# A block stack in float32r on one core: second products of three feed-forward layers rebuilt as seven-product quads, with one weight sum made by an adding transfer

## What is computed

```
# first block, layer i (0, 1): hidden width 4096
h = modulate(rmsnorm(x, norm_g[i, 1]), sh2, sc2)
x = x + gt2 * (square(relu(h @ mlp_w1[i])) @ mlp_w2[i])
# second block, both feed-forwards: hidden width 2816
def swiglu(h, w_gate, w_up, w_down):
    return (silu(h @ w_gate) * (h @ w_up)) @ w_down
x = x + 0.5 * swiglu(rmsnorm(x, ffn_norm), w_gate, w_up, w_down)
```

## Time and profile before

| | |
|---|---|
| median of 3 runs | 2538.02 us (2536.36 to 2540.02) |
| the profiled execution, its own time | 2542.36 us |
| its span, first to last instruction | 2540.6 us |
| mean granted TensorE clock | 0.988 |
| TensorE matmul busy | 2490.3 us (98%) |
| TensorE weight load busy | 2050.9 us (81%) |
| VectorE / ScalarE / GpSimd busy | 1329.9 / 908.6 / 201.8 us |

### The profile page before, as it was taken

How to read it: one execution, slowest core, us unless ns; L and a number is a source line. 1 busy time by engine, 2 the same in 40 slices (tenths; PEclk the granted TensorE clock), 3 DMA queues, 4 the chain that set the end, 5 groups by cost and what they waited for, 6 DMA issues and landing times.

```text
span 2540.6 us, 39183 instructions
## 1 busy us (share of the span) xinstructions
PE 2490.3 (98%) x16966; PEld 2050.9 (81%) x16966; DVE 1329.9 (52%) x1967; ACT 908.6 (36%) x1364; POOL 201.8 (8%) x176
## 2 busy tenths in 40 slices
PE   9999999999999999999999999999999999999998
PEld 7888888876787887888888888888668987888887
DVE  7865746647845446543444544432345745444433
ACT  4224323337633233431433322322256444322221
POOL 1000000000220000000000111000221000111100
PEclk9999999999999999999999999999999999999999
DMA  8563665622210003232222332333112422322232
GB/s 341 192 197 117 200 197 185 189 86 81 85 39 4 5 29 126 82 108 99 93 100 75 108 100 95 91 97 124 64 48 76 141 79 65 114 92 99 87 100 71
DMA packets 79725, 271.86 MB, mean 107 GB/s; under 512 B 8912, under 2 KB 11216, under 8 KB 79040
## 3 DMA queue, kind: packets, MB, share of 16 engines
q1 hardware_dynamic: 67696, 224.79, 26.9%
q0 software_dynamic: 11856, 44.55, 5.5%
HBM read 265.11 MB, written 4.19 MB: 106 GB/s over the span
## 4 chain that ended last, share of the span: by engine, by line
PE 92%; DVE 5%; ACT 2%; issue 1%; DMA 0%; SPq 0%; DVEq 0%; ACTq 0%
PE ps L624 26%; PE ps L630 22%; PE ps L628 22%; PE ps L640 3%; PE ps L643 3%; PE ps L655 1%; DVE WLs L1780 1%; PE ps L796 1%; PE ps L809 1%; DVE ada L1796 1%; PE ps L597 1%; PE ps L822 1%; PE ps L693 1%; PE ps L1119 1%; PE ps L1133 1%
## 5 line engine op out<-in xcount | busy, mean ns | idle before, releaser
L1780 DVE TENSOR_TENSOR WLs<-raw,WHs 128x1024 fp32r<-128x1024 f32 (+2 forms) x406 | 461.4, 1137 | 419.4 <-ACT WHs L1218 418.7
L624 PE MATMUL ps<-HH,WHs 128*128 128x512 f32 x1728 | 646.6, 400 | 3.7 <-DVE Pq L2332 2.1
L1218 ACT ACTIVATE WHs<-raw 128x1024 fp32r<-128x1024 f32 (+2 forms) x424 | 416.7, 984 | 550.7 <-PE ps L630 444.7
L630 PE MATMUL ps<-HH,WLs 128*128 128x512 f32 x1406 | 548.3, 390 | 1.2 <-DVE WLs L1780 1.2
L628 PE MATMUL ps<-HL,WHs 128*128 128x512 f32 x1406 | 547.7, 390 | 0.0
L624 PEld LDWEIGHTS ps<-HH,WHs 128*128 128x128 f32 x1728 | 324.9, 189 | 76.0 <-issue 11.2
L630 PEld LDWEIGHTS ps<-HH,WLs 128*128 128x128 f32 x1406 | 263.9, 188 | 57.2 <-DVE WLs L1780 1.6
L628 PEld LDWEIGHTS ps<-HL,WHs 128*128 128x128 f32 x1406 | 264.4, 188 | 53.7 <-issue 2.2
L624 PE MATMUL ps<-HM,WHs 128*128 128x512 f32 x576 | 224.1, 389 | 0.0
L628 PE MATMUL ps<-HM,WHs 128*128 128x512 f32 x576 | 224.1, 389 | 0.0
L630 PE MATMUL ps<-HM,WLs 128*128 128x512 f32 x576 | 224.1, 389 | 0.0
(11 more groups left out here) (419 smaller groups left out, 3449.0 us busy)
## 6 DMA issues: line engine op xcount, KB each, us to landing
ada<-in_adaw POOLq DMA_DIRECT2D x80, 512.0 KB, 4.5
raw<-in_f1gu_m SPq DMA_DIRECT2D x38, 512.0 KB, 3.3
raw<-in_f2gu_m SPq DMA_DIRECT2D x38, 512.0 KB, 3.2
raw<-in_mw_0b SPq DMA_DIRECT2D x32, 512.0 KB, 3.5
raw<-in_mw_1b SPq DMA_DIRECT2D x32, 512.0 KB, 3.5
raw<-in_w_in_m SPq DMA_DIRECT2D x18, 512.0 KB, 3.3
ada<-in_adaw SPq DMA_DIRECT2D x16, 512.0 KB, 15.7
raw<-in_cw_in_m SPq DMA_DIRECT2D x16, 512.0 KB, 3.4
```

Of the source, the lines that this page charges most:

```text
L624: pe.matmul(o[m], WHs[:, s, w], hi, start=k == 0, stop=False)
L630: t = pe.matmul(o[m], WLs[:, s, w], hi, start=False, stop=k == DEPTH_K[name] - 1)
L1218: act.activation(WHs[:, SLOT[v], 0:n], raw_[:, v % NRAW, 0:n], ACT.Copy).then_inc(*S.up("w_hi", ("hi", v)))
L1780: dve.tensor_tensor(WLs[:, s, 0:n], raw_[:, v % NRAW, 0:n], WHs[:, s, 0:n].bitcast(F32), SUB).then_inc(*S.up("w_lo", ("lo", v)))
```

## The change

The second products of MLP layer 1 and of the feed-forwards are done in quads: two output blocks by two halves of the tokens by two halves of the depth make a 2x2 by 2x2 block product, which is done with 7 products in place of 8 (Strassen's scheme). Each of the 7 has half of the depth and 256 tokens. The layer's hidden width is now cut into parts: `mw1_1` in 12, 10 and 10 blocks ("a", "b", "c"), each followed by its second product; `f1gu` and `f2gu` in 24 and 20 blocks. The new kind is "s"; `f2d_b` alone keeps kind "m", now with depth 10. The rest of the kernel, MLP layer 0 too, stays as it was.

- Input side: for each pair k of hidden blocks VectorE makes four combinations T1 to T4 (256 columns each), in place in the temporaries, and high and low parts of seven 256-column inputs are stored (1792 columns for a pair, before 1024).
- Weight side: the four quarters of a quad are loaded (4 transfers); of the 7 weight pieces three are quarters, three are sums by VectorE (`sum_quarters`, pieces 1, 2, 6), and piece 4 is a quarter to which a second transfer adds another one in SBUF, issued by GpSimd (`added`). Each piece gets its high and low part as before.
- Output side: each of the 7 products is added to X with its sign as soon as it is done (`draw`, 256 columns); three PSUM banks serve a quad, and four of the products are built on top of an earlier one in the same bank (`BEFORE`), after that one was drawn.
- The ring `pr` of the feed-forwards has three places in place of four, and `ending()` works on depth 10.

The code follows in this order: the tables; `fast` of TensorE; `hidden_fast` of ScalarE; the call of `sum_quarters` in VectorE's `ahead`; `combinations` and `hidden_fast` of VectorE; its `residual`, in which the products 5 and 6 of a quad close one output block each; `added` of GpSimd; `ending`.

```diff
-        ("mw1_1a", "e", 16, 8), ("mw2_1a", "m", 8, 16), ("mw1_1b", "m", 16, 8), ("mw2_1b", "m", 8, 16),
-        ("f1gu", "f", 44, 8), ("f1d", "m", 8, 22),
+        ("mw1_1a", "e", 12, 8), ("mw2_1a", "s", 8, 12), ("mw1_1b", "m", 10, 8), ("mw2_1b", "s", 8, 10),
+        ("mw1_1c", "m", 10, 8), ("mw2_1c", "s", 8, 10),
+        ("f1gu_a", "f", 24, 8), ("f1d_a", "s", 8, 12), ("f1gu_b", "m", 20, 8), ("f1d_b", "s", 8, 10),
...
-        ("f2gu", "f", 44, 8), ("f2d", "m", 8, 22)]
+        ("f2gu_a", "f", 24, 8), ("f2d_a", "s", 8, 12), ("f2gu_b", "m", 20, 8), ("f2d_b", "m", 8, 10)]
+BANK = [1, 2, 1, 3, 1, 2, 1]
+BEFORE = {2: 0, 4: 2, 5: 1, 6: 4}
+DRAWS = [(0, 0, 1), (1, 1, -1), (1, 0, -1), (0, 0, 1), (1, 1, -1), (1, 0, -1), (0, 1, 1)]
+INPUT = [0, 3, 1, 5, 2, 4, 6]
+INPUT_GROUP = [0, 2, 1, 3, 1, 2, 3]
+GROUP = [slice(0, 256), slice(256, 768), slice(768, 1280), slice(1280, 1792)]
+SUMMED = (1, 2, 4, 6)
+ADDED = (4,)
...
+            def fast(name):
+                src = name.replace("mw2", "mw1")
+                for a in range(BLOCKS[name] // 2):
+                    o = {}
+                    for i in range(7):
+                        u, b, g = FIRST[name] + 7 * a + i, BANK[i], INPUT_GROUP[i]
+                        if b not in o:
+                            o[b] = bank(name, a, b, hold=True)[:, 0:256]
+                        else:
+                            on.wait_ge(*S.at("drawn", name, a, BEFORE[i]))
+                        s, n = SLOT[u], WANT[u][4]
+                        x = slice(256 * INPUT[i], 256 * INPUT[i] + 256)
+                        on.wait_ge(*S.at("hi", u))
+                        for k in range(n):
+                            w = slice(128 * k, 128 * k + 128)
+                            on.wait_ge(*S.at("ch", src, k, g))
+                            pe.matmul(o[b], WHs[:, s, w], HT[:, 0, k, x], ...)
+                            on.wait_ge(*S.at("cl", src, k, g))
+                            pe.matmul(o[b], WHs[:, s, w], HT[:, 1, k, x], ...)
+                            on.wait_ge(*S.at("lo", u))
+                            t = pe.matmul(o[b], WLs[:, s, w], HT[:, 0, k, x], ...)
...
+            def hidden_fast(name):
+                def finish(m):
+                    k, x = m // 2, tmp_[:, m % 4]
+                    if m % 2 == 0:
+                        on.wait_ge(*S.at("t2", name, m))
+                        high(name, k, 0, x[:, early])
+                    else:
+                        on.wait_ge(*S.at("T4", name, k))
+                        high(name, k, 2, T2[:, 1])
+                        high(name, k, 1, T2[:, 0])
+                        high(name, k, 3, x)
+                def evac(m):
+                    on.wait_ge(*S.at("full", name, m))
+                    if m >= 4:
+                        on.wait_ge(*S.at("cl", name, (m - 4) // 2, 3))
+                    act.activation(tmp_[:, m % 4], taken(name, m), ACT.Relu)...
+                    if m:
+                        finish(m - 1)
+                    if m == BLOCKS[name] - 1:
+                        finish(m)
...
+                    if v + 1 < len(WANT) and WANT[v + 1][1] == "s" and WANT[v + 1][3] in SUMMED and WANT[v + 1][3] not in ADDED:
+                        sum_quarters(v + 1)
...
+            def combinations(src, k, even, odd, t1, t2, t3, t4):
+                dve.tensor_tensor(t3, odd[:, late], even[:, late], SUB)...
+                on.wait_ge(*S.at("T1", src, k))
+                dve.scalar_tensor_tensor(out=t2, in0=t1, scalar=-1.0, in1=odd[:, late], op0=MUL, op1=SUB)...
+                on.wait_ge(*S.at("T2", src, k))
+                dve.scalar_tensor_tensor(out=t4, in0=t2, scalar=-1.0, in1=odd[:, early], op0=MUL, op1=SUB)...
...
+            def hidden_fast(name):
+                def finish(m):
+                    k, x = m // 2, tmp_[:, m % 4]
+                    if m % 2 == 0:
+                        low(name, k, 0, x[:, early])
+                    else:
+                        low(name, k, 2, T2[:, 1])
+                        low(name, k, 1, T2[:, 0])
+                        low(name, k, 3, x)
+                def evac(m):
+                    k, x = m // 2, tmp_[:, m % 4]
+                    on.wait_ge(*S.at("relu", name, m))
+                    dve.tensor_tensor(x, x, x, MUL).then_inc(*S.up("v_evac", ("t2", name, m)))
+                    if m:
+                        finish(m - 1)
+                    on.wait_ge(*S.at("t2", name, m))
+                    if m % 2 == 0:
+                        if k:
+                            on.wait_ge(*S.at("cl", name, k - 1, 1))
+                        first_combination(name, k, x, T2[:, 0, late])
+                    else:
...
+                        combinations(name, k, tmp_[:, (m - 1) % 4], x, T2[:, 0, late], T2[:, 0, early], T2[:, 1, early], T2[:, 1, late])
+                    if m == BLOCKS[name] - 1:
+                        finish(m)
...
+                    if isinstance(m, tuple):
+                        draw(name, *m)
+                        for n, b in closed(m):
+                            close(name, n, b)
...
+            def added(name):
+                for a in range(BLOCKS[name] // 2):
+                    v = FIRST[name] + 7 * a
+                    on.wait_ge(*S.at("sum", v + 1))
+                    if a:
+                        on.wait_ge(*S.at("sum", v - 3))
+                    pool.dma_start(quarter(v + 4, 1), D[name][a, 2], accum_op=ADD).then_inc(*S.up("w_added", ("sum", v + 4), by=16))
...
                     for hf in range(2):
-                    for j, (u, mms, _) in enumerate(list(steps("f2d"))[-3:]):
+                    for u, mms, _ in list(steps("f2d_b"))[-2:]:
...
+                            if hf == 1 and k == 5:
+                                factors(0)
+                            if hf == 1 and k == 8:
+                                spread_end(0)
```

More of the change, by code:

```diff
@@ L70, with load_read @@
 POOLED = range(FIRST["w_in"] + 8, LAST["w_in"] + 1)
+LOADS = []
+RAW = {}
+for _u, _p in enumerate(WANT):
+    if _p[1] != "s":
+        RAW[_u] = len(LOADS)
+        LOADS.append((_u, None))
+    elif _p[3] == 0:
+        for _q in range(4):
+            RAW[_u, _q] = len(LOADS)
+            LOADS.append((_u, _q))
+HALT_LOAD = RAW[HALT]
+def load_read(load):
+    v, q = LOADS[load]
+    if q is not None:
+        return [("lo", v), ("lo", v + 4), ("lo", v + 5), ("sum", v + 6)][q]
+    return ("used" if v in WHOLE else "lo", v)
 TOKENS = [slice(0, 256), slice(256, 512)]
@@ L955, in pe_program @@
             norm("m1")
[L956 to L959 removed]
+            for part in "ab":
+                dense("mw1_1" + part, h, lambda k: ("HL", "m1", k))
+                fast("mw2_1" + part)
+            dense("mw1_1c", h, lambda k: ("HL", "m1", k))
+            if KIND["mw2_1c"] == "s":
+                fast("mw2_1c")
+            else:
+                dense("mw2_1c", hm, lambda k: ("mlo", "mw1_1c", k))
             def norm_within(tag):
@@ L1344, in within @@
                         shifted("m%d" % layer, layer, 3, i + 3)
-                for half in "ab":
-                    dense("mw1_%d%s" % (layer, half), hidden("mw1_%d%s" % (layer, half)), within if half == "a" else None)
-                    dense("mw2_%d%s" % (layer, half), residual("mw2_%d%s" % (layer, half)))
+                for part in MLP[layer]:
+                    one, two = "mw1_%d%s" % (layer, part), "mw2_%d%s" % (layer, part)
+                    dense(one, (hidden_fast if KIND[two] == "s" else hidden)(one), within if part == "a" else None)
+                    dense(two, residual(two))
             mlp(0)
@@ L1994, in within @@
                         after(i)
-                for half in "ab":
-                    dense("mw1_%d%s" % (layer, half), hidden("mw1_%d%s" % (layer, half)), within if half == "a" else after)
-                    dense("mw2_%d%s" % (layer, half), residual("mw2_%d%s" % (layer, half)), after)
+                for part in MLP[layer]:
+                    one, two = "mw1_%d%s" % (layer, part), "mw2_%d%s" % (layer, part)
+                    dense(one, (hidden_fast if KIND[two] == "s" else hidden)(one), within if part == "a" else after)
+                    dense(two, residual(two), after)
             mlp(0, ada_step)
@@ L2560, in weights @@
             def weights(first, last):
-                for v in range(first, last):
+                for r in range(first, last):
+                    v, q = LOADS[r]
                     name, kind, a, k, n = WANT[v]
```

341 lines of the change are left out of this document (247 added, 94 removed), and 3 rows, old and new, of the table RESIDUAL.

## The result

| | before | after |
|---|---|---|
| median (lowest to highest), 4 runs each | 2537.94 us (2536.36 to 2540.02) | 2573.06 us (2570.13 to 2573.78) |
| ratio to before, 95% interval | | 1.0135 (1.0122 to 1.0147) |
| profiled execution, own time / span | 2542.36 / 2540.6 us | 2573.78 / 2572.0 us |
| mean granted clock | 0.988 | 0.985 |

A forecast was written before the change was run, and what follows sets the result against it. TensorE was taken as the bound, busy for 98% of the span. The terms -26.4 + 14.2 + 22.5 + 5.2 + 1.0 + 8.0 gave +24.5: 2566.9 us against 2542.4 profiled (2562.5 against the median), 8-in-10 range 2538 to 2582.

The forecast's parts named there:

- matmul time: Second products in quads: 66 slices of depth fall from 359.0 to 332.6 us of TensorE time, -26.4 us.
- closings, mw2_1c and f1d_b: Products 5 and 6 each close a block; low parts queued behind VectorE's closes delay TensorE from the second quad, +14.2 us.
- entries, six: At each second product's start, product 2 waits for draw 0, queued behind VectorE's other work; +22.5 us including 1.5 for mw2_1a.
- eight blocks at once: In mw1_1a eight blocks end together; TensorE waits for the low part of piece 10 from 1082.5, +5.2 us.
- the end: Last norm's chain: fewer matmuls hide the spread, 1.4 us less hidden, shorter halved last block gives -0.5; +1.0 us.
- clock: Granted clock falls after long TensorE waits, 1.6 us each; five falls, +8.0 us, from 0 to 13.
- adding transfer: GpSimd's transfer adding a quarter for piece 4 lands in 4.5 us, within 7.5 or 9.2 allowed: hidden, no cost.
- The 1.5 added for mw2_1a: In the entries' sum: VectorE enters the last block of mw1_1a 1.5 us late, added to the entry into mw2_1a.
- one of my signs of being wrong: Adding transfer: the forecast would be wrong if ScalarE's high part 4 waits for the transfer.
- VectorE keeps up: Faster rival: the 26.4 gain stands, entries and closings mostly hidden; -9 us, 2529 us; chance 0.12.
- The costly late transfer: Slower rival: adding transfer takes 9.0 us, late by 1.5 in 9 quads; +13 us, 2576 us; chance 0.12.
- the last one: Rival: 256-column matmuls in quads pace slower than 0.120 us; at 0.1295 the gain is zero, 2589 us; chance 0.03.

The follow-up runs named there:

- x8: x4's order on the changed kernel, plus VectorE's closes in f1d_b put off behind draws 1 and 3 of the next quad; 2557.91 us, 1.0065 of before.
- x10: x4's order on the changed kernel, plus ScalarE's next high part ahead of its closes in f1d_b and mw2_1c; 2561.44 us, 1.0075 of before.
- x9: The edits of x8 and x10 together, on the changed kernel with x4's order; 2550.81 us, 1.0032 of before.
- x4: Changed kernel with another order at the six entries: first weight pieces and draw 0 ahead of the last inputs' parts; 2560.54 us, 1.0076 of before.
- x3: Changed kernel with six blocks side by side in mw1_1a in place of eight; 2573.73 us, 1.0122 of before.
- x1: Changed kernel without its adding transfers, piece 4 being the loaded quarter alone (wrong fourth sum); 2574.65 us, 1.0132 of before.
- x5: Changed kernel with the fourth weight sum made by VectorE in place of the adding transfer; 2574.95 us, 1.0138 of before.
- x11: Changed kernel with mw2_1c in whole blocks, mw1_1a six side by side, x4's order, both engines' closes put off in f1d_b; 2531.80 us, 0.9959 of before.
- x12_no_second_sum: x9 with VectorE's closes of mw2_1c put off too and the second sum of squares reduced to its first block; 2538.00 us, 0.9997 of before.

## Why the prediction was right in its direction, and short by 10.6 us

| term of the sum | forecast | profile after |
|---|---|---|
| matmul time | -26.4 | -26.4 |
| closings, mw2_1c and f1d_b | +14.2 | +17.5 (10.9 and 6.6) |
| entries, six | +22.5 | +19.6 |
| eight blocks at once | +5.2 | +5.4 |
| banks behind mw2_1c and f1d_b | not in it | +2.9 |
| the end | +1.0 | +1.6 |
| clock | +8.0 | +14.4 |
| adding transfer | 0 | 0 |
| sum | +24.5 | +35.0 |

The stages differ by 36.6, the medians by 35.1; 1.6 us of the stages have no term. Each matmul start right behind a wait comes about 0.1 us late as well, 0.3 us in each of three entries looked at, and that is not in the sizes above.

- **Matmul time**: right. The page counts 924 matmuls in each of the three lines of a quad, 2772 = 66 x 42, and they start 0.12 us apart between waits. The rule of the Trainium skill that was weighed (TensorE: Matmul & The Clock Gate, the section on 56 ns and 53.3 ns) would have made the pace 109 ns; no stretch shows it, the pace here is 120 ns.
- **Closings**: the mechanism is there, the size was 3.3 short, and its description was only half right. I had the low parts queued behind the closes as what TensorE waits for, 1 to 2 us on WLs. Of 3.6 us a quad in mw2_1c only 1.1 wait for a low part and 2.5 for the next quad's draw 0; in f1d_b the last link is ScalarE's high part (5.0 us in three). I had counted VectorE's work alone and left out ScalarE's queue and the bank. x8, x10 and x9 show that both queues hold it.
- **The bank behind the last quad** was a missed term: the next section's sixth block waits for the bank that the last draw frees, 1.6 us after mw2_1c and 0.9 after f1d_b, with 0.16 and 0.2 of restart.
- **Entries**: the mechanism right in five of six (x4), in mw2_1a ScalarE's high part ended the wait; each size within 1.7. The wait at product 2 is 1.8 to 2.0 us everywhere, where 2 to 4 was announced; the rest of an entry is lost in small portions in products 0 and 1. By gaps over the pace they are 2.4, 3.0, 3.0, 3.65, 4.2 and 3.4, forecast 4.1, 3.2, 3.2, 3.8, 4.4 and 3.8. The 1.5 added for mw2_1a, for VectorE's lateness in the block ahead, didn't come; that TensorE's stand of 5.4 us let VectorE catch up is argued, not shown.
- **Eight at once**: size and place right, and x3 takes it away. I had it all on the third matmul, waiting for WLs from 1082.5; it came in two portions, ScalarE's high part first.
- **The end**: TensorE's wait for the last squares is 3.0 us where it was 1.6, as counted (1.4); the sums over partitions behind it take 1.0 in place of 0.6, and the shorter half block gave back about 0.2 where I took 0.5.
- **Clock**: the step that failed most in size. A fall was priced nearly right (1.6; the stages of after, x1 and x5 give 1.5), but I counted five falls and this execution has nine more than before. Waits of 2 us with small ones of 0.2 to 0.4 ahead of them, as at 1220.9 and 1330.1, which I had called near the bound and left out, were followed by one here, and so were two closings with their two waits each, which I had not counted at all; 1080.9 and 1538.3 are double. The number is partly chance: x1_no_add, with the same waits, has five more than before (it lacks the ones behind the two norms as well) and x5_vadd seven, so this term is 7.5 to 13.5 us by the execution, and five would not have been wrong in x1's. Where waits are taken away (x3, x4, x11), falls go with them, so part of what an experiment gives back is clock; x9 gives back waits alone.
- **Adding transfer**: it takes 6.3 and not the 4.5 that I took; allowed were 7.5 and 9.2. It is hidden, as x1 shows, with about 1 us to spare in the shorter quads by my count; ScalarE waited for it twice in mw2_1b, 3.1 us in all. That was one of my signs of being wrong, and it came; but the delay reached nobody, since no wait of TensorE follows it there. My taking GpSimd's plain row was too low; the upper bound of 9.0 was too high.

The direction was no luck: each large term is there, at the place named. That the miss is only 10.6 us is partly luck, since the entries came 2.9 lower than forecast and the other terms higher. Of the rivals, "VectorE keeps up" fell, and yet its point stands: a program of the same instructions with other order does keep up (x9 in f1d_b). The costly late transfer is refuted by x1 and x5. The quads' own pace is 0.12, so the last one is refuted.

Open: whether a version with the closes of mw2_1c put off and its second sum made apart would beat x11_best. x12_no_second_sum leaves that sum out, and its seven operations of 0.62 us would have to find a place; this was not tried.

## What to carry to other kernels

A cheaper product pays only if the engines that feed it need no answer within its own length: here 26 us of matmul time cost 61 us of waits and clock, most of it at places where one engine's queue held a draw or a weight part behind work that nobody was waiting for. Before giving work up, look for the draw that frees a bank and for the weight part behind it, and put both ahead of the rest on every engine in that chain; in f1d_b one engine alone gave nothing. And count the granted clock with each short wait: where a fall followed, it nearly doubled the price of a wait of 2 us. Count the falls in each trace before comparing two of them, since they differ between executions of the same waits.

## What was not expected of the hardware

- The transfer that adds into SBUF lands in 6.3 us for 384 KB (4.4 to 6.7 over all 24), where a plain one of this size by SP takes 3.0. A part of the difference may be GpSimd's queue: its 80 plain loads of 512 KB land in 4.7 us in this trace, most of SP's in 3.4 to 3.9. The Trainium skill (DMA: Bandwidth & Descriptors, Rules for kernel authors) says that such a transfer reads its destination first and writes it later; a longer time than that of the plain load agrees with that, though no run here shows the reading.
- The clock fell to its lower level nine times more without any wait longer than 2.7 us, most often behind one of 1.8 to 2.4 with shorter ones close ahead of it. The same waits were followed by two falls, one or none in different executions (the entry into f1d_a).
- The 461 to 472 us of the RWKV stretch, in which no kernel of this study differs, move by up to 11 us from execution to execution, more than most of the effects looked for; ranges of 4 to 14 us of one kernel's executions have the same size. The clock goes with it: in the shortest (x5_vadd, 461.0 us) TensorE was at the lower level for 17.0 us of the stretch, in the longest (x12_no_second_sum, 472.2 us) for 40.9.
